# Reading the feed-forward stage's first eight row tiles, and squaring them, inside the stage before it

## What is computed

```
h = h + mix @ w_out[i]
h = h + conv_ffn(rms_norm(h, norm_ffn_g[i]), ffn_w_up[i], ffn_conv_w[i],
                 ffn_conv_b[i], ffn_w_down[i])

def conv_ffn(x, w_up, conv_w, conv_b, w_down):
    h = x @ w_up                                # 1024 -> 2 * 2816
    h = causal depthwise conv of width 3 (h) + conv_b
    val, gate = jnp.split(h, 2, axis=-1)
    return (jax.nn.gelu(gate) * val) @ w_down   # 2816 -> 1024
```

## Time and profile before

| | us |
|---|---|
| median of 3 runs (2857.01 to 2857.15) | 2857.06 |
| profiled execution, its own time | 2857.93 |
| its span in the profile | 2856.3 |
| TensorE busy | 2593.2 (91%) |
| VectorE busy | 1710.5 (60%) |
| ScalarE busy | 1369.0 (48%) |

### The profile page before, as it was taken

How to read it: one execution, slowest core, us unless ns; L and a number is a source line. 1 busy time by engine, 2 the same in 40 slices (tenths; PEclk the granted TensorE clock), 3 DMA queues, 4 the chain that set the end, 5 groups by cost and what they waited for, 6 DMA issues and landing times. The chain is left out here.

```text
span 2856.3 us, 38966 instructions
## 1 busy us (share of the span) xinstructions
PE 2593.2 (91%) x13883; PEld 2231.7 (78%) x13883; DVE 1710.5 (60%) x3358; ACT 1369.0 (48%) x2460; POOL 509.4 (18%) x309
## 2 busy tenths in 40 slices
PE   6999997999835699579999999999999999997998
PEld 5989986999834588468888878888888878885876
DVE  1110271777686777388888755578888864444333
ACT  3343332666522566355555455455555543334444
POOL 3454453766300121000000000000000000000000
PEclk9999998999968799789999999999999999998999
DMA  4665456888332354312222266642222236753221
GB/s 161 195 220 170 155 166 158 180 184 184 92 104 77 118 173 154 112 52 74 89 89 82 89 225 231 235 162 84 74 89 89 82 137 240 269 195 107 75 73 47
DMA packets 313911, 392.11 MB, mean 137 GB/s; under 512 B 22161, under 2 KB 222161, under 8 KB 310650
## 3 DMA queue, kind: packets, MB, share of 16 engines
q1 hardware_dynamic: 299850, 341.60, 39.1%
q0 software_dynamic: 13888, 48.25, 4.3%
HBM read 298.59 MB, written 95.33 MB: 138 GB/s over the span
## 5 line engine op out<-in xcount | busy, mean ns | idle before, releaser
L2365 PE MATMUL ffn_bank<-ffn_x,ffn_ring 128*128 128x512 f32 x880 | 345.9, 393 | 20.5 <-DVE ffn_ring L2159 14.3
L2366 PE MATMUL ffn_bank<-ffn_x,ffn_ring 128*128 128x512 f32 x880 | 345.1, 392 | 0.0
L2367 PE MATMUL ffn_bank<-ffn_x,ffn_ring 128*128 128x512 f32 x880 | 345.1, 392 | 0.0
L504 ACT ACTIVATE att_exps<-att_scores,att_part 128x256 f32<-128x256 f32 (+1 forms) x384 | 153.1, 454 | 125.4 <-DVE att_part L475 123.7
L2365 PEld LDWEIGHTS ffn_bank<-ffn_x,ffn_ring 128*128 128x128 f32 x880 | 167.0, 190 | 57.3 <-DVE ffn_ring L2159 9.3
L475 DVE CUSTOM_DVE_ANT_0 att_scores<-att_bank,att_bias 128x256 f32<-128x256 f32 (+1 forms) x384 | 122.5, 363 | 142.2 <-PE att_bank L422 67.7
L2432 POOL DMA_DIRECT2D ffn_act<-ffn_late x88 | 47.6, 541 | 859.5 <-DVE ffn_late L2211 859.5
L2198 DVE SCALAR_TENSOR_TENSOR ffn_strips<-ffn_strips,ffn_taps 128x512 f32<-128x512 f32 x176 | 132.0, 750 | 114.4 <-ACT ffn_strips L2009 114.4
L938 POOL TENSOR_TENSOR in_w_lo<-in_w,in_w_hi 128x2048 fp32r<-128x2048 f32 x36 | 166.0, 4612 | 183.3 <-ACT in_w_hi L821 183.3
L2366 PEld LDWEIGHTS ffn_bank<-ffn_x,ffn_ring 128*128 128x128 f32 x880 | 167.1, 190 | 35.0
L2367 PEld LDWEIGHTS ffn_bank<-ffn_x,ffn_ring 128*128 128x128 f32 x880 | 166.8, 189 | 34.9
(11 more groups left out here) (337 smaller groups left out, 6984.0 us busy)
## 6 DMA issues: line engine op xcount, KB each, us to landing
ffn_w<-in_ffn_w_up SPq DMA_DIRECT2D x88, 512.0 KB, 4.8
ffn_a_raw<-ffn_act SPq DMA_DIRECT2D x176, 256.0 KB, 5.9
ffn_w<-in_ffn_w_down SPq DMA_DIRECT2D x40, 1024.0 KB, 6.9
in_w<-in_w_in SPq DMA_DIRECT2D x36, 1024.0 KB, 6.2
ffn_act<-ffn_late POOLq DMA_DIRECT2D x88, 256.0 KB, 2.7
mixed_part<-branch_results SPq DMA_DIRECT2D x16, 792.0 KB, 5.4
z_rows<-in_result SPq DMA_DIRECT2D x80, 128.0 KB, 2.3
branch_results<-att_part SPq DMA_DIRECT2D x8, 1056.0 KB, 9.7
```

The lines of the kernel that those rows point to most:

```text
L504: nc.scalar.activation(exps[:, n % RING, m * width:(m + 1) * width], scores[:, n % RING, m * width:(m + 1) * width], ACT.Exp, bias=part[:, ...
L2365: pe.matmul(out[:, :], hi[:, k], x_hi[kind][:, k], start=(k == 0 and fresh), stop=False, skip_group_check=not fresh)
L2366: pe.matmul(out[:, :], hi[:, k], x_lo[kind][:, k], start=False, stop=False, skip_group_check=not fresh)
L2367: mm = pe.matmul(out[:, :], lo[:, k], x_hi[kind][:, k], start=False, stop=(k == KH - 1), skip_group_check=not fresh)
```

## The change

In the mixing stage's last step, SyncE waits until the raw `w_out` has been split and reads the first eight result tiles back from `after_mixers`, into the space of the raw `w_out` (`rows_ahead`). ScalarE squares and sums them behind its last two row splits. The feed-forward stage then loads no rows for its first half. Its `shared` tile now lies on the same addresses, and so kinds 1 and 2 get tiles of their own, while kinds 3, 6 and 7 use the shared one, whose rows are dead once they have been turned. VectorE scales both groups before it splits the first, the taps' copy comes after the first operands, and the exact copies of the first group (`keep_first_group`) come after VectorE's remainders, in the order of chunks 2, 3, 0, 1, counted by a new semaphore `x_kept`, on which turns, products and sums now wait. The later half takes the same order of copies, chunk by chunk. The activations that are read back have a place of their own in each half (`a_raw`).

```
 def mix_and_project(...):
@@ SyncE, behind the last step's loads
+            sp.wait_ge(w_lo_ready, KC)
+            for t in range(rows_ahead.tiles):
+                sp.wait_ge(stored[t % 2], (t // 2 + 1) * DMA)
+                sp.dma_start(rows_ahead.rows[:, t], h_tiles[t]).then_inc(rows_ahead.loaded[t], DMA)
@@ ScalarE
+            def square_ahead(t):
+                act.wait_ge(rows_ahead.loaded[t], DMA)
+                if t:
+                    act.wait_ge(rows_ahead.mean_ready, t)
+                nc.scalar.activation(squares[:, :], rows_ahead.rows[:, t], ACT.Square, scale=D ** -0.5,
+                                     accum_out=rows_ahead.mean_sq[:, t:t + 1]).then_inc(rows_ahead.mean_ready, 1)
...
+                    if last and j >= 2:
+                        for t in range((j - 2) * RING, (j - 1) * RING):
+                            square_ahead(t)
 def feed_forward(...):
+    KEEP_ORDER = (2, 3, 0, 1)
@@ SyncE
-            load_rows(0, 0)
-            load_rows(0, 1)
             load_w(0)
@@ ScalarE
-            def split_first_group(h, k):
-                one, two = turn_banks(h, 0, k)
+            def round_first_group(h, k):
                 act.wait_ge(transposed, h * TG * KH + k + 1)
-                for src, chunk, kind, kept in ((one, k, 1, 5), (two, KH + k, 2, 4)):
-                    nc.scalar.activation(exact[kept][:, k], src[:, :], ACT.Identity, scale=g_cols[:, chunk:chunk + 1])
+                for src, chunk, kind in zip(turn_banks(h, 0, k), (k, KH + k), (1, 2)):
                     nc.scalar.activation(x_hi[kind][:, k], src[:, :], ACT.Identity, scale=g_cols[:, chunk:chunk + 1]).then_inc(hi_written, 1)
+
+            def keep_first_group(h, k):
+                act.wait_ge(lo_written, h * LO_HALF + 2 * k + 2)
+                for src, chunk, kept in zip(turn_banks(h, 0, k), (k, KH + k), (5, 4)):
+                    nc.scalar.activation(exact[kept][:, k], src[:, :], ACT.Identity, scale=g_cols[:, chunk:chunk + 1]).then_inc(x_kept, 1)
...
-            for t in range(TILES):
-                square(0, 0, t)
             root(0, 0)
+            root(0, 1)
             act.wait_ge(gain_loaded, DMA)
             for k in range(KH):
-                split_first_group(0, k)
-            for t in range(TILES):
-                square(0, 1, t)
-            root(0, 1)
+                round_first_group(0, k)
+            for k in KEEP_ORDER:
+                keep_first_group(0, k)
...
                             if h + 1 < HALVES and p == 1 and f in TURN_AT:
-                                split_first_group(h + 1, TURN_AT.index(f))
+                                round_first_group(h + 1, TURN_AT.index(f))
+                                keep_first_group(h + 1, TURN_AT.index(f))
@@ VectorE
+                dve.wait_ge(x_kept, (h + 1) * 2 * KH if h else 2 * KEEP_ORDER.index(k) + 2)
                 nc.vector.scalar_tensor_tensor(t1, one[:, :], scale_one, t1, ALU.mult, ALU.subtract).then_inc(x_summed, 1)
...
             scale_rows(0, 0)
+            scale_rows(0, 1)
             dve.wait_ge(gain_loaded, DMA)
...
@@ TensorE, turn()
                 if h == 0 and grp == 1 and k < 2:
-                    pe.wait_ge(lo_written, 2 * (k + 2) + 2)
+                    pe.wait_ge(x_kept, 2 * KEEP_ORDER.index(k + 2) + 2)
@@ TensorE, multiply()
+                if h == 0 and j < 3:
+                    pe.wait_ge(x_kept, 2 * KEEP_ORDER.index(0 if j == 0 else 1) + 2)
```

More of the change, by code:

```diff
@@ L27, with __init__ @@
 LINE = 512
+class RowsAhead:
+    def __init__(self, nc, keep, tiles):
+        self.mean_sq = keep.sb("ahead_mean_sq", [P, tiles])
+        self.loaded, self.mean_ready = keep.sems("ahead_loaded", tiles), keep.sem("ahead_mean_ready")
+        self.tiles, self.rows = tiles, None
 class Stage:
@@ L1812, in rows_of @@
         def rows_of(h, grp, t):
-            if h == 0 and grp == 1:
-                return late.rearrange("p t n -> p (t n)")[:, t * D:(t + 1) * D] if t < 2 else plain[:, (t - 2) * D:(t - 1) * D]
+            if h == 0:
+                return rows_ahead.rows[:, grp * TILES + t]
             return plain[:, 2 * EDGE + t * D:2 * EDGE + (t + 1) * D]
-        def rows_count(h, grp):
-            return (h + 1) * DMA
         def turn_banks(h, grp, k):
@@ L2223, in _ @@
                 split_first_group(0, k)
-            dve.wait_ge(taps_turned, 1)
-            nc.vector.tensor_copy(taps[:, :, :], bank[3][:, 0:N_TAPS * 2 * F].rearrange("p (n f) -> p n f", f=2 * F)).then_inc(taps_ready, 1)
-            scale_rows(0, 1)
             sum_weights(0, 0, 0)
@@ L2230, in _ @@
                 split_operand(0, j)
+            dve.wait_ge(taps_turned, 1)
+            nc.vector.tensor_copy(taps[:, :, :], bank[3][:, 0:N_TAPS * 2 * F].rearrange("p (n f) -> p n f", f=2 * F)).then_inc(taps_ready, 1)
             for k in range(KH):
@@ L2719, in hybrid_block @@
         with Stage(nc, "mixers") as st:
-            w_out = st.sb("w_out", [P, KC, D])
+            w_out = st.sb("w_out", [P, KC, D], align=LINE)
+            shared_at = nc.sbuf_base - KC * D * 4
+            rows_ahead.rows = st.over("rows_ahead", [P, KC, D], F32, shared_at)
             w_out_loads = chunk_loads(st, "w_out", w_out, w["w_out"])
```

64 lines of the change are left out of this document (40 added, 24 removed).

## The result

The changed kernel takes 2838.3 us (median of six runs, 2837.1 to 2840.1), against 2857.1 us before (six runs, 2855.2 to 2860.3). The ratio is 0.9934, 95% interval 0.9921 to 0.9947: faster by 18.8 us. The forecast was 2840.3 us, with 2837 to 2848.5 as its range. The profiled execution has a span of 2837.5 us, 18.8 less than before.

A forecast was written before the change was run, and what follows sets the result against it. TensorE was 91% busy, with VectorE's chain deciding the boundary. Its second group moving from 1213.64 to 1196.85 saves 16.8 us: 2857.93 becomes 2841.1, and 0.87 lower for the timed median gives 2840.3 us, range 2837 to 2848.5.

The forecast's parts named there:

- Step 1: Feed-forward opening: row loads and eight squares hide in the mixing stage, moving VectorE's epsilon 10.0 us earlier.
- Step 2: Opening: VectorE scales both groups from 1177.4 to 1184.2; TensorE turns first tiles from 1180.9 at half clock.
- Step 3: Opening: gain transfer takes 7.3 us, landing at 1185.1; ScalarE's rounding waits, VectorE's remainders run 1185.8 to 1191.05.
- The bounds: Opening: gain lands between 1180.1 and 1185.1; at 1180.1 remainders start at 1184.3 and the saving is 18.3 us.
- Steps 4 and 5: Opening: weight sums end at 1193.7, late copies make VectorE wait 1.5 us, second group starts at 1196.85.
- one turn that may come late: TensorE's products and turns before VectorE's second group: one turn late by 0 to 2.07 us, taken as 0.
- Later half: Later half: ScalarE's copies wait for VectorE four times, 1.1 us each; 3.4 us of slack, so nothing.
- The starved gain: Opening: VectorE's scales hold up GpSimd's gain issue; saving 11.3 to 15.4 us, time say 2844; chance 0.27.
- The early reads: Mixing stage: row reads delay the last tile's inputs 4.3 us; saving 12.5, time 2844.6 us; chance 0.08.
- Late code: Opening: first instructions behind a branch come 0 to 3.7 us late; chance 0.05 together with a late turn.
- The clock rival: Feed-forward stage: TensorE's clock drops; 34 us more at 0.50 eat the saving, 50 give 2865; chance 0.03.
- it does nothing: Boundary: loads land late, squares still run there, opening keeps its start; 2856 to 2857 us; chance 0.02.

The follow-up runs named there:

- Reads late: Changed kernel with the eight row reads held until the mixing stage's last add but one; 2845.3 us, ratio 0.9957 to the kernel before.
- squares at the opening: Changed kernel with the eight row squares moved back to the feed-forward opening, reads still in the mixing stage; 2844.9 us, ratio 0.9953 to before.
- Weights behind the gain: Changed kernel with SyncE's loads at the opening held until the gain has landed, gain still issued by GpSimd; 2842.1 us, ratio 0.9941 to before.
- Copies between: Changed kernel with the opening's exact copies made between ScalarE's roundings again, tile by tile; 2841.4 us, ratio 0.9941 to before.
- first pair of traces: First traces of the kernel before and the changed kernel; 1679.0 and 1659.6 us from the opening's start to the span's end.
- second pair: Both kernels traced once more, word for word; 1678.3 us before and 1659.7 us after, from the opening's start to the span's end.
- later half as before: Changed kernel with the later half's first group copied as before, copy and rounding alternating on ScalarE; 2838.0 us, ratio 0.9936 to before.
- amid the scales: Changed kernel with the gain's load held on GpSimd until VectorE's first scale of the opening is finished; 2838.2 us, ratio 0.9931 to before.
- gain from SyncE: Changed kernel with the feed-forward gain's load issued by SyncE as its first transfer instead of by GpSimd; 2839.0 us, ratio 0.9934 to before.

## Why the prediction was right, and where it was off

Forecast places stand here against the changed kernel's, both from the opening's start (the forecast's 1177.29).

| place | forecast | measured |
|---|---|---|
| VectorE's epsilon | 0.1 | 0.05 |
| first turn | 3.6 | 3.95 |
| second scales end | 6.9 | 7.20 |
| gain landed | 7.8 | 6.4 |
| remainders start | 8.5 | 7.27 |
| remainders end, sums start | 13.8 | 12.54 |
| VectorE's wait for the operand | 1.5 long | 1.50 long |
| second group starts | 19.6 | 18.25 |

Step 1 (loads and squares hide): right. The first epsilon stands where it was put, the squares ended at 1164.8 (forecast 1166.1). *Reads late* shows the cover by removing it, *squares at the opening* that the squares cost 5.0 us where they are not covered. Those runs don't split the other 13 us one by one; the copy order is 2.3 of them, and what the loads alone are worth no run shows.

Step 2 (both groups scaled, turns at half clock): 0.3 to 0.4 us too early. VectorE's first scale took 1.21 us, not 0.75, because of GpSimd's issue beside it: with the gain issued by SyncE it is 0.75 again. The forecast had considered that pair of engines and had the loser wrong.

Step 3 (the gain): **this is the mis-sized term.** I took the transfer's own 7.3 us; it took 5.9. 7.3 had been measured behind 4 MB of row loads, which this very change removes; the transfer now stood behind 1 MB of up weights. *Weights behind the gain* (2.9 us) shows that the other loads make the difference; that the 1.4 us between 7.3 and 5.9 are the row loads' is read from this, not shown by a run of its own. The bounds held it, and the 1.2 us by which the remainders started early is nearly the whole miss of the second group's place, 1.3. With the gain at 6.4 and the scales over at 7.20, the gain set the remainders' start by 0.15 us at most. The forecast's "15 us of slack" is misread besides: from issue to first use it was 15.2 us before, of which the transfer took 7.3.

Steps 4 and 5 (sums, late copies, a wait of 1.5 us): right to 0.1 us, from the remainders' end to the second group 5.71 us, forecast 5.8. *Copies between* shows the gain from the order: the sums 3.87 us earlier, 2.26 us kept.

What VectorE gains moves TensorE by as much: 36.35 to 18.25 is 18.10, and the third wait's end moved by 18.11. The forecast's clause on one turn that may come late cost nothing. To the span's end it is 19.4 us in the first pair of traces and 18.7 in the second (1678.3 less 1659.65).

**How much of 18.8 was foreseen.** The forecast was a saving of 16.8 us; 18.8 lies inside the range of times, but just above the band of savings (15.5 to 18.5) that was called the forecast. The 2.0 us more are three things. The opening gave 1.3 more (18.1), mostly the gain. The changed kernel's start came 0.61 later, which took that much off and is no part of the change. And 1.3 came behind the second group, which the forecast had at nothing. Followed along VectorE's operations, the lead of the first pair changes nearly only at the two places where the clock differed: 18.1 up to the third wait, 17.2 behind it, 17.6 from about 700 us on, 19.1 behind the wait near 2313 (2330 before), 19.4 at the end. In the second pair it goes 18.3, 19.2, 19.3, 19.0, 18.7. So what both pairs share is the opening's part; the rest differs from execution to execution, and that it added to the saving here and did not take from it is luck.

Later half: nothing, as forecast, shown by *later half as before*.

The rivals. The starved gain (0.27) fell: the issue takes 0.92 us between VectorE's scales as well, the landing did not move, and with SyncE's loads held back it came 2.9 us after an issue that had the same scales beside it (3.19 us for four). By the Trainium skill (SBUF — State Buffer, "SBUF: two separate sides") a VectorE operation in a two-port mode keeps GpSimd from writing its descriptors. The same section of the Trainium skill also says that whichever comes first keeps the pair of ports for its whole instruction. The traces agree that the two engines meet and that the order decides: the lengthened scale is each time the one that starts while GpSimd's issue runs, by 0.39 to 0.46 us. In the other order (amid the scales, where a scale had run for 0.39 us when the issue began) they show no delay of the DMA. The early reads (0.08) fell: the last tile's operations start without a wait. Late code (part of 0.05) fell: VectorE's first instruction stands 0.05 us behind SyncE's. The clock rival (0.03) fell: the granted clock is 0.99 from 1240 to 2590 us in both kernels. (Its threshold was put too low: 34 us at 0.50 take 0.013 from a mean over 1350 us, so the saving would be eaten at about 0.98, not 0.97.) That it does nothing is excluded by the interval.

Not settled: what sets the clock's level at the two places, the 0.4 us that the first pair gains on the way to 700 us, and why *reads late* is 1.3 us longer from start to end than the changed kernel's second trace, with the same 0.97 near 2313.

## What to carry to other kernels

A stage boundary whose next stage starts with loads and a reduction is a place to read ahead into memory that the old stage has finished with: look for an engine that sleeps there and for a tile that is dead, and check how far ahead the data are written. Once the opening is short, what had slack in it is next (here a gain vector of 4 KB), and such a load's duration must be taken with the bytes that will stand ahead of it after the change, not with those before. Count times from a common event near the change, since this kernel's stages ahead moved the boundary by some us from one execution to the next, more than most of the effects looked for.

## What the runs showed of the hardware that was not expected

- A 4 KB load's landing depends on what the DMA engines already hold: issued by GpSimd it took 7.3 us beside 4 MB of row loads, 5.9 beside 1 MB of weights, 4.6 when issued 1.26 us later beside the same loads, 2.9 with nothing ahead; from SyncE, first in line, 2.2.
- A DMA issue on GpSimd lengthens the VectorE scale (128x1024, float32) that starts while it runs from 0.75 to 1.14 or 1.21 us; a scale already under way is not lengthened, and the issue stays at 0.92.
- The same matmuls of the same kernel took 9.30 us at a granted clock of 0.68 in one execution and 7.90 us at 0.81 in another.
- Eight reads of 512 KB held back to the end of the mixing stage landed 7.7 us (median) after their issue, and the stage's last store 7.6 us after its own, for 2.9 in the trace of *gain from SyncE*.
